# A gather kernel for one core: the rows of v are fetched and summed four steps behind the rows of u

## What is computed

```python
def block(xb):                                   # 128 tokens, xb is (128, 1024)
    qh = jnp.einsum('td,de->te', xb, w_q).reshape(PEER_BLOCK, PEER_HEADS, 2, PEER_KEY_DIM // 2)
    s = jnp.einsum('thcd,hcnd->thcn', qh, sub_keys).astype(jnp.float32)
    ...
    top_s, sel = lax.top_k(cand, PEER_TOPK)
    eidx = jnp.take_along_axis(cidx, sel, axis=-1)   # 8 heads x 16 experts = 128 per token
    g = jax.nn.softmax(top_s, axis=-1)
    act = jax.nn.gelu(jnp.einsum('td,thkd->thk', xb, u_tab[eidx]).astype(jnp.float32), approximate=False)
    return jnp.einsum('thk,thkd->td', (g * act).astype(xb.dtype), v_tab[eidx])
```

## Time and profile before

| | |
|---|---|
| time, median of three runs | 3998.46 us |
| the profiled execution | 4045.73 us, its span 4044.0 us |
| projections and u part of the first tile alone | to 715 us of the span |
| eight periods with a u and a v part | 715 to 3836 us |
| last period, v part alone | 3836 to 4026 us, then the tail |
| bytes moved by DMA | 1389.41 MB, 1215.35 MB of it by the gathers' queue |

### The profile page before, as it was taken

The page is one execution under the profiler, slowest core; times in us unless marked ns, Lnnn a source line. Parts: engine busy times, 40 slices in busy tenths (PEclk is TensorE's granted clock), DMA queues, the critical chain, the costliest instruction groups (busy, mean ns, idle before and its releaser), DMA issues.

```text
span 4044.0 us, 48466 instructions
## 1 busy us (share of the span) xinstructions
PE 2780.5 (69%) x16300; PEld 1405.1 (35%) x16300; DVE 2535.5 (63%) x6869; ACT 1054.3 (26%) x2881; POOL 2261.6 (56%) x2365
## 2 busy tenths in 40 slices
PE   7999999677577747774777488658774674333365
PEld 6845644333234314441443144224331331000021
DVE  2445657775876678758776787687767556544400
ACT  3312212323232223222322323233322111110121
POOL 1102443666666666656666666665656666666665
PEclk9999999778677867776778687868875575555567
DMA  7645798999999999999999999999999999999998
GB/s 204 187 142 163 259 344 272 375 374 389 375 373 363 388 371 378 372 365 358 359 375 372 366 366 376 387 376 351 384 360 357 373 391 351 368 369 365 366 362 314
DMA packets 545781, 1389.41 MB, mean 344 GB/s; under 512 B 61289, under 2 KB 225313, under 8 KB 545537
## 3 DMA queue, kind: packets, MB, share of 16 engines
q0 software_dynamic: 335024, 1215.35, 79.9%
q1 hardware_dynamic: 198288, 161.34, 12.5%
q10 hardware_dynamic: 12224, 9.63, 0.9%
HBM read 1352.93 MB, written 33.04 MB: 343 GB/s over the span
## 4 chain that ended last, share of the span: by engine, by line
PE 16%; POOL 11%; DMA 11%; DVE 11%; issue 8%; another core or an unknown queue 5%; ACT 1%; DVEq 0%; ACTq 0%; POOLq 0%
POOL d_vb L1726 6%; DMA d_ub<-in_peer_u_dram,d_eid 5%; PE d_pY L1756 5%; POOL d_ub L1707 5%; DMA d_vb<-in_peer_v_dram,d_eidT 5%; DVE d_ub L1920 5%; PE d_pS L855 2%; PE r_pB L1456 2%; PE d_pS L941 1%; PE d_pS L921 1%; PE d_pS L880 1%; POOL d_ub L1726 1%; PE r_pB L1471 1%; PE d_pS L869 1%
## 5 line engine op out<-in xcount | busy, mean ns | idle before, releaser
L1920 DVE CUSTOM_DVE_ANT_0 d_ub<-d_ub,d_pX 128x1024 f32<-128x1024 f32 x1024 | 1242.5, 1218 | 645.9 <-DMA d_ub<-in_peer_u_dram,d_eid 515.9
L1707 POOL DMA_INDIRECT d_ub<-in_peer_u_dram,d_eid x1152 | 1135.6, 986 | 868.8 <-DVE d_hdot L1920 379.7
L1756 PE MATMUL d_pY<-d_vb,d_dg 128*32 128x256 f32 x8768 | 958.6, 515 | 851.2 <-DMA d_vb<-in_peer_v_dram,d_eidT 547.7
L1726 POOL DMA_INDIRECT d_vb<-in_peer_v_dram,d_eidT x1096 | 1043.2, 952 | 768.0 <-PE d_pY L1756 260.0
L1756 PEld LDWEIGHTS d_pY<-d_vb,d_dg 128*32 128x32 f32 x8768 | 256.2, 127 | 1459.1 <-issue 1273.7
L1795 ACT ACTIVATE d_dg<-c_late_sb,d_wgtT 128x32 f32<-128x32 f32 x1152 | 333.8, 314 | 1259.8 <-PE d_pY L1756 675.2
L707 PE MATMUL d_pX<-d_wq,d_vb 128*128 128x512 f32 (+3 forms) x1536 | 475.2, 462 | 17.8 <-DMA d_vb<-in_w_in_dram 9.7
L707 PEld LDWEIGHTS d_pX<-d_wq,d_vb 128*128 128x128 f32 x1536 | 271.9, 201 | 184.1 <-issue 117.5
L1456 PE MATMUL r_pB<-r_side,c_small_sb 128*128 128x128 f32 (+15 forms) x1152 | 175.7, 319 | 20.1 <-issue 14.0
L1920 DVE CUSTOM_DVE_ANT_0 d_ub<-d_ub,d_vb 128x1024 f32<-128x1024 f32 x128 | 155.2, 1220 | 49.6 <-DMA d_ub<-in_peer_u_dram,d_eid 46.4
L1456 PEld LDWEIGHTS r_pB<-r_side,c_small_sb 128*128 128x128 f32 x1152 | 174.7, 241 | 33.3 <-issue 23.7
(11 more groups left out here) (282 smaller groups left out, 3544.8 us busy)
## 6 DMA issues: line engine op xcount, KB each, us to landing
d_vb<-in_w_in_dram SPq DMA_DIRECT2D x68, 512.0 KB
d_ub<-in_peer_u_dram,d_eid POOLq DMA_INDIRECT x1152
d_vb<-in_peer_v_dram,d_eidT POOLq DMA_INDIRECT x1096
r_side<-in_cache_k_dram SPq DMA_DIRECT2D x16, 1024.0 KB
r_side<-in_cache_v_dram SPq DMA_DIRECT2D x16, 1024.0 KB
d_wo<-in_w_out_dram SPq DMA_DIRECT2D x6, 2048.0 KB, 9.4
d_wo<-in_peer_w_q_dram SPq DMA_DIRECT2D x4, 2048.0 KB, 8.9
scratch_h<-t_shared SPq DMA_DIRECT2D x9, 512.0 KB
```

Source lines behind the costliest of these rows:

```text
L1707: pool.indirect_dma_start(out=ub[:, g % R, :], out_offset=None, in_=io["peer_u"][0], in_offset=off).then_inc(u_in[g % R], 16)
L1726: pool.indirect_dma_start(out=to, out_offset=None, in_=io["peer_v"][0], in_offset=off).then_inc(landed, 16)
L1756: m = nc.tensor.matmul(pY[q * QT:(q + 1) * QT, g % 2, :], dg[:, n % DG, :], rows[:, q * QD:(q + 1) * QD], start=k % QT == 0, stop=k % QT = ...
L1920: nc.vector.tensor_tensor_reduce(out=ub[:, g % R, :], in0=ub[:, g % R, :], in1=xflat if i else xn_of(0), scale=1.0, scalar=0.0, op0=ALU.mu ...
```

## The change

The v part runs `LAG` = 4 steps later in every engine's program. POOL's step `k` of period `i` issues u gather `k` and v gather `k-4`; the first four steps of a period fetch the last four v rows of the tile before. There is a short extra period with four v gathers. PE's `weigh_rows`, ACT's `column` and DVE's `residual` move with it. The chain that turns the weights is spread over the four steps in between: the second `weigh` on DVE to step 1, `turn_weights` on PE to step 2, the copy to `wgtT` and the first six columns on ACT to step 3. On ACT `copy_x` now stands ahead of `gelu`. The last residual, the squares and the rest up to the store of y move from steps 0, 1, 3, 4, 5, 8 to steps 5, 5, 7, 8, 9, 12; `load_xs` stays at step 20. The mixer's wait for the turned weights moves from its start to its first `turn`.

```diff
                 if g == 0:
                     if U + u:
                         pe.wait_ge(o_done, U + u)
+                    if u == 0 and i >= 2:
+                        pe.wait_ge(wT_done, i - 1)
                     if u == 0 and i >= 3:
                         pe.wait_ge(froot_done, i - 2)
...
-            if i >= 2:
-                pe.wait_ge(wT_done, i - 1)
...
             else:
                 pe.wait_ge(in_oa, 16)
+                pe.wait_ge(wT_done, i - 1)
                 pe.wait_ge(froot_done, i - 2)
...
+        LAG = 4
...
-                for i in range(NT + 1):
-                    for k in range(NEXP):
+                for i in range(NT + 2):
+                    for k in range(NEXP if i <= NT else LAG):
...
-                        if i:
-                            n = NEXP * (i - 1) + k
-                            if k == 0:
-                                pool.wait_ge(ids_done, 2 * i)
+                        n = NEXP * (i - 1) + k - LAG
+                        if n >= 0:
+                            j = n // NEXP
+                            if n % NEXP == 0:
+                                pool.wait_ge(ids_done, 2 * (j + 1))
...
-                            off = bass.IndirectOffsetOnAxis(ap=eidT[:, (i - 1) % 3, k:k + 1], axis=0)
+                            off = bass.IndirectOffsetOnAxis(ap=eidT[:, j % 3, n % NEXP:n % NEXP + 1], axis=0)
...
-                        if 1 <= i <= NT:
-                            if k == 0:
-                                turn_weights(i - 1)
-                            weigh_rows(i - 1, k)
-                        if i >= 2 and k == 3:
+                        if 1 <= i <= NT and k == 2:
+                            turn_weights(i - 1)
+                        n = NEXP * (i - 1) + k - LAG
+                        if 0 <= n < NEXP * NT:
+                            weigh_rows(n // NEXP, n % NEXP)
+                        if i >= 2 and k == LAG + 3:
...
                             if k == 0:
-                                gelu(j, CUT, NEXP)
                                 if i < NT:
                                     copy_x(i)
+                                gelu(j, CUT, NEXP)
+                            if k == LAG - 1:
                                 act.wait_ge(wT_psum, j + 1)
                                 nc.scalar.activation(wgtT[:, j % 2, :], pT[:, 0:P], ACT.Copy).then_inc(wT_done, 1)
                                 act.wait_ge(wT_done, j + 1)
                                 for c in range(AHEAD):
                                     column(j, c)
-                            if k + AHEAD < NEXP:
-                                column(j, k + AHEAD)
+                            if 0 <= k - LAG and k - LAG + AHEAD < NEXP:
+                                column(j, k - LAG + AHEAD)
                             if k == 20:
                                 load_xs(j)
                         if i >= 2:
-                            if k == 1:
+                            if k == LAG + 1:
                                 squares(i - 2)
-                            if k == 4:
+                            if k == LAG + 4:
                                 mean_root(i - 2)
-                            if k == 8:
+                            if k == LAG + 8:
                                 store_y(i - 2)
...
-                        if 1 <= i and k == 0:
-                            finish(i)
-                        if 1 <= i <= NT and k % QT == 1 and k > QT:
-                            residual(i - 1, k // QT - 1)
+                        if 1 <= i <= NT and k == 1:
+                            weigh(i - 1, 1, CUT, NEXP)
+                        if 1 <= i <= NT and (k - LAG) % QT == 1 and k - LAG > QT:
+                            residual(i - 1, (k - LAG) // QT - 1)
+                        if i >= 2 and k == LAG + 1:
+                            residual(i - 2, 3)
...
-                            if k == 5:
+                            if k == LAG + 5:
                                 last_norm(i - 2)
```

More of the change, by code:

```diff
@@ L1895, in last_norm @@
                                                        ALU.mult, ALU.mult).then_inc(y_done, 1)
-                def finish(i):
-                    if i <= NT:
-                        weigh(i - 1, 1, CUT, NEXP)
-                    if i >= 2:
-                        residual(i - 2, 3)
                 for k in range(FIRST, 0):
```

## The result

| | before | changed |
|---|---|---|
| median of 22 runs each, us | 4006.23 | 4022.43 |
| lowest and highest, us | 3992.4, 4024.11 | 4010.62, 4033.85 |
| ratio to before | | 1.0036 [1.0026, 1.0046] |
| profiled execution, us | 4045.73 | 4023.99 |

The change costs 14 us by the ratio. That is within 0.5% of no change, but the interval excludes no change, and 4022 lies above the range of 3953 to 4010. What the two profiles say of single waits can still be read.

What follows compares the result with a forecast made beforehand. The prediction took the DMA, busy 0.99 at 371 GB/s, to bound the kernel. Terms -11 (stalls at period starts), +3 (start of period 1) and 0 (other moves) gave -8 us, from 3998.5 to 3990 us, range 3953 to 4010.

Steps and rivals of the forecast that it cites:

- What bounds the kernel: Joint periods: DMA busy 0.99 at 371 GB/s, no compute engine at its limit; a stall costs only if the DMA runs dry.
- Stalls at the eight starts: Starts of periods 2 to 9: spreading the weight-turning chain over four steps removes dips of 2.8 us at four starts, -11 us.
- Start of period 1: First four steps issue u gathers alone, the four v gathers come behind the last period: -1 to +6 us, taken as +3.
- Moves with one answer: Other moved pieces (table loads, store of y, v pieces in mid-period) keep every pair of waits as before: 0 us each.
- The dip to 293 GB/s: DMA rate of 293 and 297 GB/s for 10 us after the fifth period start, behind PE's 5.94 us wait; worth 2.8 us.
- A: Rival: period-start stalls count in full, gain bounded by 43 us at the residual's and root's waits, 3955 us; chance 0.24.
- B: Rival: mixer's first `turn` makes PE wait for the later root in five mixers, +30 and +3, 4031 us; chance 0.14.
- C: Rival: DMA's mean rate is fixed, dips only move, so only the start counts, +3, 4001 us; chance 0.12.
- The range: Whole program: 3953 to 4010 us; the forecast's own range was 3977 to 4004, with chance 0.50.
- My own last line: Sign: a change of pace in the middle of the periods, far from any start, would speak against the whole reading.
- the windows of rows 4: 40 us trace windows around the eight period starts: DMA at 368 to 403 GB/s, read as hardly noticing the stalls.

Runs made afterwards that it cites:

- e3: Kernel before, with DVE adding a tile's last residual group at step 1 of the next period instead of step 0: 3826.1 us, ratio 1.0007.
- e14: Changed kernel, with the first 32 products of the recurrence in each period from the second on placed behind the step's scores on PE: 3824.7 us, ratio 0.9999.
- e15: Kernel before, with the same 32 products placed behind the scores on PE: 3824.4 us, ratio 1.0002.
- e8: Kernel before, no lag, with only the final norm moved from step 5 to 9 and the store from 8 to 12: 3839.7 us, ratio 1.0040.
- e7: Changed kernel, with the final norm at step 14 in place of 9 and the store at 17 in place of 12: 3837.5 us, ratio 1.0034.
- e9: Kernel before, no lag, with the final norm at step 14 and the store at 17: 3826.6 us, ratio 1.0009.
- e16: Changed kernel run again without an edit, as the measure for e14 and e15: 3837.8 us, ratio 1.0033.
- e6: Changed kernel run again without an edit, as the measure for other experiments: 3840.1 us, ratio 1.0041.
- e0: Kernel before run again without an edit, for a second profile and the spread: 3824.5 us, ratio 1.0002.
- e11: Kernel before, with four times six extra PE products ahead of the first recurrence block of each period from the second on: 3832.8 us, ratio 1.0029.
- e13: Kernel before, with extra PE products ahead of all four heads' recurrence blocks in each period from the second on: 3835.4 us, ratio 1.0033.
- e12: Kernel before, with the final norm at step 9 and extra PE products ahead of each period's first recurrence block: 3821.5 us, ratio 1.0000.
- e10: Changed kernel, with four times six extra PE products in steps 9 to 12 of each period from the second on: 3823.2 us, ratio 1.0006.

## Why the prediction was wrong

**What bounds the kernel** held: DMA near its limit at 0.99, and only stalls that last until the DMA runs dry count. e3 is the cleanest case: 31 us more waiting, nothing lost.

**Stalls at the eight starts, -11 us.** No such gain is shown. With the scores' wait out of the way, changed and before differ by -1 us (e14 and e15, ratios 0.9999 and 1.0002, each uncertain by 0.001, 4 us). The start of period 1 accounts for -1 us, which leaves about 0 for the stalls, uncertain by 5 us. The waits themselves did shrink: ACT's for the root, 17.8 us before and 5.6 at its longest, came to 6.7 us and 2.5 at its longest, and DVE's for the residual fell from 61 to 42 us. No time came of it, and the dip from which the -11 was sized was still there in the fifth period, 308 and 321 GB/s. So the step from "this wait goes" to "the dip behind it goes" failed too.

**Start of period 1, +3 us,** was about -1 (-6.0 in period 1, +4.8 behind the last one), at the lower bound of -1 to +6. I took the saving from the first four steps alone and missed that the steps behind them run faster as well.

**Moves with one answer, 0 us each: this is the step that failed.** "In the middle of a period every pair of waits is as before" assumed that only the relative order of the moved pieces counts, and the term asked only what would be late of the moved work itself, not who waits for whatever stands beside it at its new place. It left out the final norm, 1.85 us of DVE from step 5 to 9, and it left out that other v rows now stand beside steps 9 to 12 on PE. Each alone is enough for the loss (e8, and e7 against e9). PE runs dry ahead of L1457, its granted clock falls to 0.50, the block takes up to 7.00 us in place of 3.7, and DVE waits for the scores behind it, 24 to 29 us at the four middle starts. That costs 15 us in e8 and 13 us with the lag (e16 less e14, same chip). How the lag makes PE run dry with the norm out of the way is read from e7's rows, not shown by a run of its own. The sum is then -1 us for all else and +13 to +15 for this wait, 12 to 14 us; the comparison gave 14.

**What I had seen and passed over.** DVE's longest wait in the joint periods of before was the 9.84 us at L1055, with 132 GB/s behind it. I had filtered DVE's waits for lines that the change touches. The dip to 293 GB/s, which I put down to the exponentials behind the root, is not this wait: it is over at 2332 us, and DVE's wait for the scores at that start, 3.20 us, ends at 2346 us. What makes that dip no run shows.

**Rivals.** A (3955) did not come: the residual's wait fell and no time was won. B (4031) is nearest in kind, a new wait of the mixer in place of the old ones, and the measured time lies in its interval, but that is in part luck: it named PE waiting for the root, and the list of PE's waits has none for it; the one that came is DVE's for the scores. C (4001) was right that these stalls have nothing to give, within 5 us, and had nothing of the new wait.

**The range** left out a cost that appears away from the moved instructions. Its lower end is also off by its own terms: 24 + 1 us from 3998.5 is 3973, not 3977. My own last line, that a change of pace far from any start would speak against the reading, did not come true: steps 40 to 127 are as fast as before. The loss sits in steps 12 to 24, some 35 to 75 us behind a period's first u gather, and the windows of rows 4 cover the first 40 us. Steps 4 to 19 of the middle periods take 3.2 to 3.3 us each in e6 against 2.7 to 2.9 in e0.

Open: why e11 and e13 lose 0.3% where e12, with e11's products and the norm at 9, loses nothing; what part of the loss is the slow block's own; and on the chip of the comparison the link rests on the traces' likeness, since the experiments ran on others.

e14 doesn't beat the kernel before, nor does any other. The lag and the kernel before are worth the same once the block stands behind the scores.

## What to carry to other kernels

Ask of a moved instruction not only who waits for it, but who waits for whatever stands behind it on its engine; a step number further on may be the one place in the period where another engine has no slack. Where PE shares its queue between a long block and a short product for which another engine waits, put the short one first: the short one then no longer depends on how fast the block runs. Sort all waits by length before filtering them for the lines of the diff; DVE's waits at four middle starts were worth more than all that the change aimed at. And follow a saving to the end of its period before counting it, and check that the profiled execution of a kernel has the loss that its median has.

## What the runs showed of the hardware

An engine's idle time was not free although it was not the bottleneck. The same 32 products took 3.64 to 3.74 us at granted clock 1.00 and 7.00 us at 0.50, and which one they got depended on how busy PE had been just before: idle for over 3 us in e8, or busy 0.57 and 1.09 us of 2 in e7, and it got 0.50; busy without a gap since 2238 us in e0, even at 0.50, and it got 1.00. 24 extra products per period took the changed kernel from a ratio of 1.0041 (e6) to 1.0006 (e10), each against the kernel before on its own chip; the same products made the kernel before slower, by 0.29% (e11).

The Trainium skill (TensorE: Matmul & The Clock Gate, Part 1: The HAM clock gate) says that the array runs at 1.2 GHz by default and that activity releases 2.4 GHz. The rows agree, with 7.00 us against 3.64 us for the same products. Under HAM oscillation, the same page of the Trainium skill describes how waits for DMA between bursts of products throttle the array again, so that the next burst starts at the low clock. e7's rows agree in kind: PE ran single v rows between waits for DMA of 0.61 and 1.43 us, and the block behind them ran at 0.50.
